# Second layer's prompt stage: levels 5 to 7 in one group behind the cross values, and the near blocks copied in halves by ScalarE and VectorE

## The reference, cut to what matters

```python
def hgrn2_block(S, q, k, i, log_f):
    A = jnp.cumsum(log_f, axis=1)
    diff = A[:, :, None] - A[:, None, :]
    decay = jnp.exp(jnp.where(causal[None, :, :, None, None], diff, -jnp.inf))
    attn = jnp.einsum('bthk,btshk,bshk->bhts', q, decay, k)
    o = jnp.einsum('bhts,bshv->bthv', attn, i) + jnp.einsum('bthk,bhkv->bthv', q * jnp.exp(A), S)
    a_last = A[:, -1]
    S_new = jnp.exp(a_last)[..., None] * S + jnp.einsum('bshk,bshv->bhkv', k * jnp.exp(a_last[:, None] - A), i)
    return S_new, o
```

## Time and profile before

| | |
|---|---|
| median of 3 runs | 2603.52 us (2592.67 to 2609.27) |
| the profiled execution's own time | 2583.49 us |
| its span | 2581.8 us |
| mean granted TensorE clock | 0.983 |
| PE busy over the span | 2429.1 us (94%) |
| DVE busy | 1859.0 us (72%) |
| ACT busy | 1469.0 us (57%) |
| POOL busy | 354.3 us (14%) |
| from the first to the last tile's value transposes in this stage | 2144.97 to 2520.92 us of the span, 14 tiles |

### The profile page before, as it was taken

One profiled execution on the slowest core, in us unless ns is written; L12 is line 12 of the kernel. 1 busy time (PEld: TensorE's weight loads), 2 busy tenths in 40 slices (PEclk: granted clock), 3 DMA queues, 4 the chain that ended last, 5 costly groups with the idle time before them and its releaser, 6 DMA issues. The chain is left out here.

```text
span 2581.8 us, 61131 instructions
## 1 busy us (share of the span) xinstructions
PE 2429.1 (94%) x23733; PEld 2126.8 (82%) x23733; DVE 1859.0 (72%) x3580; ACT 1469.0 (57%) x3368; POOL 354.3 (14%) x584
## 2 busy tenths in 40 slices
PE   6999999999869999999998899999999979999997
PEld 3899999999746677777776898989999967777775
DVE  5899787787545555555555999778797767777774
ACT  3564666665434555555554565666765556666663
POOL 1332000000002111111111232000000021112111
PEclk9999999999889999999999999999999989999999
DMA  5787887779783322222223788778779693443431
GB/s 176 259 292 251 276 281 235 242 242 303 184 254 99 87 76 69 83 76 61 83 74 140 244 282 267 251 238 248 245 241 289 230 279 105 127 133 116 130 118 64
DMA packets 402564, 480.62 MB, mean 186 GB/s; under 512 B 40516, under 2 KB 249212, under 8 KB 402280
## 3 DMA queue, kind: packets, MB, share of 16 engines
q1 hardware_dynamic: 385592, 416.51, 51.3%
q0 software_dynamic: 14848, 55.45, 6.2%
q10 hardware_dynamic: 1840, 4.75, 0.7%
HBM read 329.78 MB, written 151.56 MB: 186 GB/s over the span
## 5 line engine op out<-in xcount | busy, mean ns | idle before, releaser
L1354 PE MATMUL pj_acc<-x_hi,pj_wh 128*128 128x256 f32 (+1 forms) x3136 | 919.0, 293 | 38.6 <-DVE pj_wl L461 36.0
L1354 PE MATMUL pj_acc<-x_hi,pj_wl 128*128 128x256 f32 (+1 forms) x3136 | 906.7, 289 | 0.0
L1354 PE MATMUL pj_acc<-x_lo,pj_wh 128*128 128x256 f32 (+1 forms) x3136 | 906.6, 289 | 0.0
L454 ACT ACTIVATE pj_wh<-pj_wt 128x512 fp32r<-128x512 f32 x728 | 456.8, 635 | 354.8 <-DMA pj_wt<-tsum 263.5
L1354 PEld LDWEIGHTS pj_acc<-x_hi,pj_wh 128*128 128x128 f32 x3136 | 597.7, 191 | 53.9 <-DVE pj_wl L461 51.3
L1354 PEld LDWEIGHTS pj_acc<-x_hi,pj_wl 128*128 128x128 f32 x3136 | 598.1, 191 | 0.0
L1354 PEld LDWEIGHTS pj_acc<-x_lo,pj_wh 128*128 128x128 f32 x3136 | 597.7, 191 | 0.0
L461 DVE SCALAR_TENSOR_TENSOR pj_wl<-pj_wt,pj_wh 128x512 fp32r<-128x512 f32 x728 | 511.7, 717 | 116.1 <-ACT pj_wh L454 102.8
L1205 DVE TENSOR_TENSOR pj_out<-pj_out,pj_acc 128x512 f32<-128x512 f32 (+1 forms) x448 | 319.8, 714 | 85.4 <-PE pj_acc L1354 60.6
L2452 ACT COPY pb_pt<-pb_TP 128x384 f32<-128x384 f32 (+2 forms) x272 | 107.3, 394 | 312.9 <-PE pb_TP L2182 238.2
L2343 DVE COPY pb_pt<-pb_TP 128x256 f32<-128x256 f32 (+2 forms) x266 | 115.8, 435 | 143.1 <-PE pb_TP L2179 132.9
(11 more groups left out here) (318 smaller groups left out, 3876.2 us busy)
## 6 DMA issues: line engine op xcount, KB each, us to landing
pj_wt<-tsum SPq DMA_DIRECT2D x588, 256.0 KB, 3.5
proj<-pj_out SPq DMA_DIRECT2D x112, 512.0 KB, 4.1
tsum<-pj_wt SPq DMA_DIRECT2D x140, 256.0 KB, 3.3
pj_wraw<-in_w_in_dram POOLq DMA_DIRECT2D x24, 1024.0 KB, 6.4
tsum<-pj_wraw SPq DMA_DIRECT2D x56, 256.0 KB, 4.4
hg_x<-x_mid SPq DMA_DIRECT2D x17, 512.0 KB, 3.6
out_dram<-hg_x POOLq DMA_DIRECT2D x17, 512.0 KB, 3.0
pb_gate<-proj SPq DMA_DIRECT2D x16, 512.0 KB, 4.9
```

The source lines that it names most:

```text
L454: nc.scalar.mul(self.hi[j][:], self.source(step), scale_of(c, self.l)).then_inc(self.s_hi, 1)
L1354: ins = nc.tensor.matmul(BANK[j][:, 0:n], a[j][:, k], x.of(y, p, j)[:, k], start=(k == 0 and i == 0), stop=(k == 3 and i == 2))
```

## The change

On TensorE, `cross_values(t)` and chunk 8 of the projection go ahead of `level(t, 5)`, so that levels 5, 6 and 7 stand behind each other, with chunk 9 after them.

The four copies of `near` are shared: ScalarE keeps the blocks 0 and 1 and VectorE has the blocks 2 and 3, in a function of its own, `copy_near`, that signals a new semaphore, `s_low`. `outputs` waits for it, and `place(t, 0)` of the next tile too. On ScalarE the two copies go ahead of `carry(t, 7)`, and `copy_half` goes behind it. On VectorE `place(t, 5)` goes behind `step(t, 6)`, and the new copies come next, ahead of `final_mean`, `step(t, 7)` and all that is made for the next tile.

```diff
--- before.py
+++ after.py
@@ -2522,7 +2522,8 @@
     s_ldf, s_init = sem("hg_ldf"), sem("hg_init")
     s_ldx = [sem(f"hg_ldx{i}") for i in range(2)]
     s_stx = [sem.software(f"hg_stx{i}") for i in range(2)]
-    s_q1, s_st, s_ca, s_lv, s_cp, s_c6, s_c7, s_full = (sem(f"hg_{n}") for n in ("q1", "st", "ca", "lv", "cp", "c6", "c7", "full"))
+    s_q1, s_st, s_ca, s_lv, s_cp, s_c6, s_c7, s_full, s_low = (
+        sem(f"hg_{n}") for n in ("q1", "st", "ca", "lv", "cp", "c6", "c7", "full", "low"))
     s_tv, s_ia, s_id, s_kn, s_kna, s_knd, s_kv, s_state = (
         sem(f"hg_{n}") for n in ("tv", "ia", "id", "kn", "kna", "knd", "kv", "state"))
     s_hv, s_sq, s_ms, s_rs, s_o, s_ot, s_y, s_yh, s_yl = (
@@ -2827,6 +2828,7 @@
 
                     if c == 0:
                         pe.wait_ge(s_full, t + 1)
+                        pe.wait_ge(s_low, t + 1)
                         pe.wait_ge(s_c6, t + 1)
                         pe.wait_ge(s_c7, t + 1)
                         pe.wait_ge(s_ia, t + 1)
@@ -2872,10 +2874,9 @@
                     level(t, 4)
                     project(t, 5, 7)
                     cross_turn(t)
-                    project(t, 7, 8)
+                    project(t, 7, 9)
+                    cross_values(t)
                     level(t, 5)
-                    cross_values(t)
-                    project(t, 8, 9)
                     level(t, 6)
                     level(t, 7)
                     project(t, 9, LATE)
@@ -2976,8 +2977,17 @@
                         dve.wait_ge(s_cp, MASKED * t + i)
                     else:
                         wait(dve, s_full, t)
+                        wait(dve, s_low, t)
                     nc.vector.copy_predicated(blocks(near[:]), masks[:, i:i + 1].bitcast(U32).to_broadcast([P, MG, BLK]),
                                               blocks(SC[bank(t, i)][:, 0:MG * BLK])).then_inc(s_cp, 1)
+
+                def copy_near(t):
+
+                    dve.wait_ge(s_cp, MASKED * (t + 1))
+                    for b in range(2, 4):
+                        rows = slice(b * BLK, (b + 1) * BLK)
+                        ins = nc.vector.tensor_copy(three(am[rows])[:, :, rows], blocks(near[rows]))
+                    ins.then_inc(s_low, 1)
 
                 def least(t, c):
 
@@ -3023,8 +3033,9 @@
                     step(t, 5)
                     inverse(t)
                     add(t, 0)
+                    step(t, 6)
                     place(t, 5)
-                    step(t, 6)
+                    copy_near(t)
                     if t:
                         final_mean(t - 1)
                     step(t, 7)
@@ -3113,7 +3124,7 @@
                 def copy_near(t):
 
                     act.wait_ge(s_cp, MASKED * (t + 1))
-                    for b in range(4):
+                    for b in range(2):
                         rows = slice(b * BLK, (b + 1) * BLK)
                         ins = nc.scalar.copy(three(am[rows])[:, :, rows], blocks(near[rows]))
                     ins.then_inc(s_full, 1)
@@ -3146,10 +3157,10 @@
                     carry(t, 5)
                     probs(t)
                     carry(t, 6)
+                    copy_near(t)
+                    carry(t, 7)
                     copy_half(t)
-                    carry(t, 7)
                     copy_far(t)
-                    copy_near(t)
                     if t + 1 < NT:
                         carry(t + 1, 1)
                     keys(t)
```

## The result

The changed kernel takes 2608.2 us (median of 8 runs, 2598.83 to 2611.73), the kernel before 2596.19 (8 runs with the three shown above). The ratio is 1.0042, with a 95% interval of 1.0023 to 1.0062: slower by 10.9 us (6.0 to 16.1; the two medians lie 12.0 apart). That the forecast of 2608.2 is met to the tenth is luck: it was set on a median of 2603.52, which with more runs fell by 7. The difference was forecast at +4.7, with +0.4 to +8.7 as bounds, and is +10.9, more than twice as much.

The account below looks back on a forecast made before the run. TensorE was taken to bound the kernel, VectorE and GpSimd nearly late. Terms +8.0 (14 tiles x 0.57), -1.1 and -2.2 made +4.7 us: 2608.2 on the median of 2603.52, range 2594 to 2614.

Parts of the forecast that it names:

- TensorE bounds the kernel before, with the other tracks close behind: Kernel before: TensorE busy 26.30 of 26.67 us a tile; VectorE had 0.11 us to spare, GpSimd about 0.05.
- Now chunk 8 starts at 2242.07 and takes 3 x 0.23 = 0.70, since it has full-width work on both sides.: TensorE's new order: chunk 8 follows chunk 7 directly; chunk 9 comes 0.21 us earlier, outputs 0.58 with ScalarE's wait gone.
- The sum: Whole kernel: 14 tiles +8.0 us, tiles 0 and 15 -1.1, unexplained gaps -2.2, in all +4.7 (+0.4 to +8.7).
- ScalarE's part: ScalarE with two near copies left: its last copy lands about 2247.75, before TensorE's outputs at 2248.16, so their wait goes.
- The wait of about 1.1 us forecast for the first chunk: TensorE at the next tile's first projection chunk: stands about 1.1 us, the gate 0.57 late and its outputs 0.58 earlier.
- The copies on VectorE at 0.26 each, one after the other: VectorE's two new 32 x 192 copies: 0.26 us each (0.16 to 0.35), the second starting only after the first ends.
- `final_scale` 0.73 later, the gate 0.57 later, 27.2 us a tile: End of a tile: VectorE's copies delay `final_scale` 0.73 us, and through GpSimd `gate(t, 0)` by 0.57; a tile takes 27.2.
- GpSimd last: GpSimd, held by the store's wait for `final_scale`, comes free 0.73 us later at 2252.43, after the mean near 2252.2.
- The two unexplained gaps are absorbed: Two tiles' TensorE gaps of 1.5 to 1.7 us precede a chunk where it now stands 1.1 us anyway: -2.2 us.
- TensorE's gain: Rival: TensorE's 0.58 us is kept in all 16 tiles, -9.3 us, giving 2594.2; chance 0.15.
- the granted clock: Rival: TensorE's new gap lowers the clock in each of 15 tiles, +25 us, about 2633 with the +4.7; chance 0.03.
- the group saves nothing: Rival: no step between widths saved by grouping levels; TensorE has 0.37 us, not 0.58, same time; inside the forecast's 0.62.

Follow-up runs that it names:

- before_early: Kernel before with only `final_mean`, `final_scale` and the store moved up in the lists: median tile 26.57 us against 26.62, ratio 0.9991.
- steps_first: Changed kernel with VectorE's `place(t, 5)` and its two copies behind `final_mean` and `step(t, 7)`: median tile 26.94 us against 27.77, ratio to the kernel before 1.0033.
- copies_twice: Changed kernel with two more VectorE copies of the same shape, into a tile nothing reads: median tile 28.13 us against 27.77, ratio to the kernel before 1.0057.
- change_early: Changed kernel with `final_mean`, `final_scale` and the store of the tile before moved up: median tile 26.81 us, ratio to the kernel before 1.0011.
- sums_first: Changed kernel with GpSimd's gate products ahead of the store: median tile 27.74 us against 27.77, ratio to the kernel before 1.0058.
- halves_alone: Changed kernel with TensorE's list as in the kernel before: median tile 26.06 us against 26.62 in the kernel before, ratio 0.9987.
- halves_early: Changed kernel with TensorE's old list, and `final_mean`, `final_scale` and the store moved up: median tile 25.90 us, ratio to the kernel before 0.9954.

## Why the prediction was right, and where not

- **TensorE bounds the kernel before, with the other tracks close behind.** Right that it bounds (before_early changed next to nothing). The slack of the others was 0.45 us, not 0.11 and 0.05: from `final_scale` to the gate pass 7.38 us before and 6.93 in the changed kernel.
- **"Now chunk 8 starts at 2242.07 and takes 3 x 0.23 = 0.70, since it has full-width work on both sides."** This is the step that failed. Chunk 8 is the first of the second half of the columns: `project` has `wait(pe, s_xadd, 2 * job + half)` where `s == 0`, and the bank OP is free only when VectorE's `add` has read the first half. In the old order level 5 and the cross values stood between chunks 7 and 8 and hid that `add` (0.69 us and the step to it). The line was in the code and I read the order of the matmuls alone. The sum put this wait at nothing. Chunk 8 started 0.93 us later than worked out, level 5 1.03 later (2244.92 on the old scale for 2243.89). With chunk 8 behind the levels again and all else as changed, a tile is 1.43 us shorter (chunk8_behind).
- **ScalarE's part**: right. The outputs don't wait for it. But TensorE didn't start them 0.58 earlier; it was 0.26 later, by chunk 8's wait. The wait of about 1.1 us forecast for the first chunk came out at 0.97 by luck: a gate that is 1.21 late instead of 0.57, and a TensorE that is 0.26 late instead of 0.58 early.
- **The copies on VectorE at 0.26 each, one after the other**: right (0.52 for two, 0.55 to the next start).
- **`final_scale` 0.73 later, the gate 0.57 later, 27.2 us a tile**: the mechanism right, the size wrong by the step above: 1.66, 1.21 and 27.77. The two errors went opposite ways: 0.93 more than forecast at `final_scale`, less the 0.29 of slack that I had under-read (0.45 for 0.16), is the 0.64 more at the gate. In the median tile steps_first (-0.83) and copies_twice (+0.36) show that VectorE's list carried it, and change_early that 0.2 us over the old tile would remain if it didn't. 27.77 lies above the forecast's upper bound too, 0.90 over 26.62.
- **GpSimd last**: right, by 0.27 us, though in the kernel before it had more to spare than the 0.05 I took; but nothing is to be had from it alone (sums_first).
- **The two unexplained gaps are absorbed**: in the main, in this one profile. It has one tile of 28.50, 0.73 above the others; before, the two stood 1.6 to 1.7 above. What the gaps are stays open, and the profiles of steps_first and halves_alone have tiles 4 us above the others.
- **The sum**: +4.7 forecast, +10.9 measured (6.0 to 16.1), +14.0 in the stage of the two profiles. In the profiles the 14 tiles give +12.6: 1.15 more in each are +16.1 (8.0 forecast), less 3.5 from the longer tiles (2.2 forecast). Tiles 0 and 15 and the end of the stage give +1.4, where I had -1.1.
- **The rivals**: TensorE's gain was not kept; the granted clock stayed at 1.00 over these tiles (windows 2160:2547 of the profile after) with gaps of 0.78 and 0.97. That the group saves nothing was nearly so: 0.09.

By the median tile, the halves alone would have been a gain of 0.56 us a tile on the kernel before. Of the 1.71 us between that and the changed kernel, which loses 1.15, chunk 8's place ahead of the levels makes 1.43 and the group itself about 0.3.

## What to carry to other kernels

When a matmul is moved earlier, look at what it waits for and at what had covered that wait: here the group that used to stand between two accumulations in one bank was hiding the read-out of that bank. Then follow the delay through the lists of the other engines: a wait at the head of a list moves everything behind it, and one 1.28 us operation with no reader nearby (`final_scale`) is better put into a gap that is there already (halves_early against halves_alone: 25.90 for 26.06). Slack where two tracks meet can't be read off the gap in front of the join: an engine that itself waits there for someone else shows less than it has.

## What the runs showed of the hardware

GpSimd's products slow VectorE's two-input operations and are slowed by them. VectorE's 128x384 multiplication takes 0.55 us with no products beside it, and two 128x128 products on GpSimd take 1.00 in the changed kernel, where they start beside VectorE's small 128x192 operation (0.35 long). In sums_first they start beside `final_scale`, and take 2.08, and two 128x384 multiplications 0.82 each. In the kernel before, the 128x192 operation beside the products took 0.62 (2250.77 in the timeline), and in three tiles of chunk8_behind 1.22. No run has the products with VectorE idle. The Trainium skill (SBUF — State Buffer, Who interferes with whom) says that a VectorE instruction with two SBUF inputs contends with a GpSimd instruction that reads SBUF. The trace agrees.

VectorE's copy of 32x192 from SBUF to SBUF takes 0.24 to 0.26 us (copies_twice), ScalarE's 0.35 (changed kernel, `copy_near`).
